# Gates from two fp32r parts, the mLSTM denominator as a value column, zero-filled differential queries, norm rows without diagonals

## The chip, the cores and the metric

One core of a Trainium2 chip. The metric is the device time of one execution in microseconds. An execution is about 2 us longer than its span from the first to the last instruction.

## What is computed

Two transformer blocks one behind the other, for one sequence of 512 tokens of width 1024, in float32. The weights are read once from HBM. Cut to what the change touches:

```python
# first block, layer A: mLSTM with a memory attention beside it
h = rmsnorm(x, norm_g)
qk, v, o, z, i_pre, f_pre, mq, mz = split_cols(h @ w_in, [...])     # i_pre, f_pre: 4 columns each
...
num = einsum("bhts,bhsv->bhtv", p, vb) + ...                         # 4 heads of 256
den = jnp.sum(p, axis=-1) + ...
h_out = num / jnp.maximum(jnp.abs(den), jnp.exp(-m_t))[..., None]
...
# second block: differential attention, 4 heads of two 64-wide components
s = einsum('bqhcd,bkhcd->bhcqk', q_blk, k) * scale
p = softmax(where(mask, s, NEG_BIG))
a = p[:, :, 0] - lam * p[:, :, 1]
...
return rms_norm(x, g_final)
```

Each layer begins with `rmsnorm(t, g) = t * rsqrt(mean(t*t) + EPS) * g`.

## The kernel before, in words

Activations stand with features on the partitions. Every large product is a sum over k-tiles of 128 features. Weights and activations are fp32; for the products each is split in two fp32r parts, hi (a copy that rounds) and lo (the rest), and one product row group is three fp32r matmuls: hi by hi, hi by lo, lo by hi (`product_rows`, L1237 to L1239 for products whose output has tokens on the partitions, L1242 to L1244 for features). Weights come in 256 to 512 KB parts by SP's DMAs into two raw slots; for each part ScalarE writes hi (L1536) and DVE lo (L1901) into one of three split slots. Everything else on PE is plain fp32.

A planner (`Plan`, `order_of_work`) lays out one list of steps in Python before anything is recorded: product row groups with their evictions, and between them side steps from two lanes, each with a lag in the planner's own clock (`lag`, `side_ns`). `tensor_program`, the ScalarE and DVE programs and POOL's then each walk this list and record their share, with semaphore waits between them.

The stages are A (the mLSTM layer), B (latent attention), C (differential attention and a pooling branch), D (cross attention), E (MLP) and the end. The steps that matter here:

- **Norms** (a, mem, b, c, m2, d, e, f): `sqa` squares a tile of x on ScalarE (L1577), `sqp` adds it to a running sum on POOL (L2454). `nsq` is four one-column fp32 matmuls (L1269) that give the sum of squares of each token. `nsum` is two small DVE operations and a power of -1/2 on POOL (L2445). `ndiag` writes four diagonal blocks with the roots on DVE (L1904), `nrow` is one fp32 matmul of ones with these (L1277), which gives the roots as a row on all partitions; ScalarE copies it to SBUF (L1580). For the last norm, f, POOL adds only tiles 1 to 3; `nsq f` takes the other four tiles as extra blocks (20 matmuls). `store` multiplies x, the gain and the row on DVE (L1910) and SP writes the result out.
- **gate0 to gate3**: the eight columns i_pre and f_pre, as 64 zero-filled columns of fp32 weights `gw`, two k-tiles per step, two fp32 matmuls per k-tile (L1297, L1298). They run between row groups of product qkA0. `gateP` and `gateA` make cumulative sums and maxima of the gates on DVE and ScalarE, `gateT` turns them on PE (L1308). After them on DVE come the evictions and the causal convolution of head 0, then the splits and the output gates of ozA0.
- **hval** (head h, token tile i): the denominator as (i+1) matmuls of the probabilities with a column of ones (L1358), the numerator as (i+1) with 256 value columns (L1360), into one bank.
- **dsc** (head h, query tile j), 16 units in stage C: for each of two components one score matmul on 64 partitions (L1428) and one mask matmul of 128 bf16 columns (L1216). Scores of 128 partitions with the same form stand in stage B (L1396).
- **rtp**: turns the rotated queries and keys of a head; ScalarE copies them out (L1791).
- **gate_loads** and **late**: side loads, the first in stage A after product mv0, the second at the start of stage C.

## Time and profile before

| | us |
|---|---|
| three runs | 1663.5, 1662.62, 1660.24 (median 1662.62) |
| the profiled execution | 1657.19 |
| its span | 1655.4 |
| PE busy in it | 1590.4 (96%) |
| DVE busy | 910.1 (55%) |
| ScalarE (ACT) busy | 692.8 (42%) |
| POOL busy | 150.6 (9%) |
| mean granted TensorE clock | 0.987 of 2.4 GHz |

The busy time of PE is that of matmuls whose ends are modelled and which overlap; the distance between starts, or the chain of waits, gives their pace. An fp32 matmul leaves two records.

### The profile page before, as it was taken

Reading aid. Unit: us, or ns where it says so; the run is one execution under the profiler, and the core shown is the slowest. Engines: PE = TensorE matmul, PEld = TensorE weight load, DVE = VectorE, ACT = ScalarE, POOL = GpSimd, SP = SyncE. Lnnn points to the kernel's source line nnn. Section 1 sums busy time; section 2 is a strip of 40 time slices with the busy share of each in tenths; the row PEclk is TensorE's granted clock in tenths of the full one; section 3 lists DMA queues with packets and bytes.
Section 4 is the critical chain, followed back from the end, with each engine's and each line's share of the span. In section 5 each row is a group of like instructions: output and inputs, shape, how many; then the busy total and the mean of one; then the engine's idle time right before and its main releaser. Section 6 shows DMA issues by size and latency. Waiting matters only on the chain.

```text
span 1655.4 us, 19328 instructions
## 1 busy us (share of the span) xinstructions
PE 1590.4 (96%) x7194; PEld 1250.7 (76%) x7194; DVE 910.1 (55%) x1856; ACT 692.8 (42%) x1587; POOL 150.6 (9%) x115
## 2 busy tenths in 40 slices
PE   7999999999999998999899999999999999999996
PEld 5867777777898876666577777688877888888885
DVE  6457485648555566466448556765554544444342
ACT  6633342323346656456334344343343433333241
POOL 3002020202110000000013000011001100000001
PEclk9999999999999999999999999999999999999998
DMA  6522121323324321012124221124232333333231
GB/s 191 151 60 77 51 77 52 93 61 125 105 75 135 87 63 47 26 53 77 51 66 127 77 65 51 52 89 140 72 108 77 98 93 102 92 99 101 90 102 51
DMA packets 90109, 141.06 MB, mean 85 GB/s; under 512 B 7456, under 2 KB 37536, under 8 KB 90016
## 3 DMA queue, kind: packets, MB, share of 16 engines
q1 hardware_dynamic: 89296, 139.02, 27.7%
q8 instruction: 57, 0.93, 0.2%
q10 hardware_dynamic: 720, 0.81, 0.2%
q14 instruction: 36, 0.29, 0.1%
HBM read 137.71 MB, written 2.10 MB: 84 GB/s over the span
## 4 chain that ended last, share of the span: by engine, by line
PE 78%; DVE 12%; ACT 5%; issue 3%; DMA 2%; POOL 0%; SPq 0%; POOLq 0%; ACTq 0%; DVEq 0%
PE banks L1237 16%; PE banks L1239 16%; PE banks L1238 16%; PE banks L1242 5%; PE banks L1244 5%; PE banks L1243 5%; DVE sb_w_split L1901 3%; DVE sb_arena L1901 3%; DVE sb_arena L1910 2%; PE banks L1200 2%; ACT sb_junk L1504 1%; PE banks L1412 1%; PE banks L1397 1%; PE banks L1360 1%; DVE sb_arena L1904 1%
## 5 line engine op out<-in xcount | busy, mean ns | idle before, releaser
L1901 DVE TENSOR_TENSOR sb_w_split<-sb_raw,sb_w_split 128x512 fp32r<-128x512 f32 (+4 forms) x530 | 342.9, 689 | 374.3 <-ACT sb_w_split L1536 373.6
L1536 ACT ACTIVATE sb_w_split<-sb_raw 128x512 fp32r<-128x512 f32 (+4 forms) x530 | 287.9, 592 | 418.7 <-PE banks L1239 314.3
L1237 PE MATMUL banks<-sb_actA,sb_w_split 128*128 128x512 f32 x672 | 278.1, 414 | 0.3 <-ACT sb_arena L1594 0.3
L1239 PE MATMUL banks<-sb_actA,sb_w_split 128*128 128x512 f32 x672 | 263.8, 393 | 0.0
L1238 PE MATMUL banks<-sb_actA,sb_w_split 128*128 128x512 f32 x672 | 263.0, 391 | 0.0
L1237 PE MATMUL banks<-sb_actB,sb_w_split 128*128 128x512 f32 (+1 forms) x640 | 249.4, 390 | 4.3 <-DVE sb_w_split L1901 2.2
L1239 PE MATMUL banks<-sb_actB,sb_w_split 128*128 128x512 f32 (+1 forms) x640 | 243.2, 380 | 0.0
L1238 PE MATMUL banks<-sb_actB,sb_w_split 128*128 128x512 f32 (+1 forms) x640 | 243.2, 380 | 0.0
L1242 PE MATMUL banks<-sb_w_split,sb_actA 128*128 128x512 f32 (+1 forms) x384 | 155.6, 405 | 15.8 <-DVE sb_w_split L1901 9.4
L1244 PE MATMUL banks<-sb_w_split,sb_actA 128*128 128x512 f32 (+1 forms) x384 | 149.8, 390 | 0.0
L1243 PE MATMUL banks<-sb_w_split,sb_actA 128*128 128x512 f32 (+1 forms) x384 | 149.6, 390 | 0.0
L1237 PEld LDWEIGHTS banks<-sb_actA,sb_w_split 128*128 128x128 f32 x672 | 127.5, 190 | 28.0 <-issue 3.6
L1239 PEld LDWEIGHTS banks<-sb_actA,sb_w_split 128*128 128x128 f32 x672 | 126.8, 189 | 27.8
L1238 PEld LDWEIGHTS banks<-sb_actA,sb_w_split 128*128 128x128 f32 x672 | 127.4, 190 | 25.2 <-issue 1.2
L1237 PEld LDWEIGHTS banks<-sb_actB,sb_w_split 128*128 128x128 f32 x640 | 121.3, 190 | 29.9 <-issue 3.6
L1238 PEld LDWEIGHTS banks<-sb_actB,sb_w_split 128*128 128x128 f32 x640 | 121.4, 190 | 22.9 <-issue 1.4
L1239 PEld LDWEIGHTS banks<-sb_actB,sb_w_split 128*128 128x128 f32 x640 | 121.2, 189 | 22.9
L2454 POOL TENSOR_TENSOR sb_arena<-sb_arena 128x512 f32<-128x512 f32 x41 | 61.2, 1492 | 696.5 <-ACT sb_arena L1577 693.9
L2445 POOL TENSOR_TENSOR sb_small<-sb_small,sb_cons 128x4 f32<-128x4 f32 (+3 forms) x30 | 42.4, 1414 | 674.8 <-DVE sb_small L1907 617.3
L1242 PEld LDWEIGHTS banks<-sb_w_split,sb_actA 128*128 128x128 f32 x384 | 73.3, 191 | 31.4 <-issue 10.5
L1200 PE MATMUL banks<-sb_cons,sb_arena 128*128 128x128 f32 x460 | 77.3, 276 | 19.6 <-DVE sb_arena L1904 9.9
L1200 PEld LDWEIGHTS banks<-sb_cons,sb_arena 128*128 128x128 f32 x460 | 57.5, 141 | 43.7 <-DVE sb_arena L1904 14.0
(185 smaller groups left out, 2076.5 us busy)
## 6 DMA issues: line engine op xcount, KB each, us to landing
sb_raw<-in_a_w_in SPq DMA_DIRECT2D x66, 256.0 KB, 3.0
sb_raw<-in_w_up SPq DMA_DIRECT2D x32, 512.0 KB, 3.7
sb_raw<-in_w_down SPq DMA_DIRECT2D x32, 512.0 KB, 3.7
sb_raw<-in_w_in SPq DMA_DIRECT2D x24, 512.0 KB, 3.6
sb_raw<-in_mem_w_kv SPq DMA_DIRECT2D x16, 512.0 KB, 3.8
sb_raw<-in_w_ckv SPq DMA_DIRECT2D x16, 512.0 KB, 3.8
sb_raw<-in_a_w_in SPq DMA_DIRECT2D x15, 512.0 KB, 3.8
sb_raw<-in_a_w_out SPq DMA_DIRECT2D x12, 512.0 KB, 3.8
```

What stands on the lines that cost most here:

```text
L1200: t = pe.op.transpose(v.ps[0:rows, place.bank, n * P:(n + 1) * P], block, v.ident)
L1237: pe.op.matmul(out, hi[:, cs], x.hi(k), start=i == 0, stop=False)
L1238: pe.op.matmul(out, hi[:, cs], x.lo(k), start=False, stop=False)
L1239: t = pe.op.matmul(out, lo[:, cs], x.hi(k), start=False, stop=last_i)
L1242: pe.op.matmul(out, x.hi(k)[:, cs], hi, start=i == 0, stop=False)
L1243: pe.op.matmul(out, x.hi(k)[:, cs], lo, start=False, stop=False)
L1244: t = pe.op.matmul(out, x.lo(k)[:, cs], hi, start=False, stop=last_i)
L1536: act.op.activation(hi[:, cs], raw[:, cs], ACT.Copy).then_inc(act.mark(m("w_hi"), 2 * n + part + 1), 1)
L1901: dve.op.tensor_tensor(out, a, b, op).then_inc(dve.mark(*mark) if mark else dve.tick(), 1)
L1910: dve.op.scalar_tensor_tensor(out=out, in0=a, scalar=s, in1=b, op0=op1, op1=op2).then_inc(dve.mark(*mark) if mark else dve.tick(), 1)
L2445: pool.op.tensor_tensor(v.stat(root, n), v.stat(mean, n), v.con("minus_half", 0, n), ALU.pow).then_inc(m.at("rstd", step)[0], 1)
L2454: pool.op.tensor_tensor(total, total, v.square_of(norm, n)[1], ALU.add).then_inc(signal, 1)
```

## The change

- Gates: `gw` is loaded as 64 dense numbers per partition by one DMA. POOL zero-fills two fp32r arrays of 1024 columns (`gw_parts`, in the free places 8 and 9 of actB), the new step `gate_split` puts hi (ScalarE) and lo (DVE) of the weights into them. Each k-tile is three fp32r matmuls, 24 in all. The planner's cost of a gate step falls from 3440 to 1360.
- hval: the values of a head are stored as 257 columns, the last of them ones, written once by POOL (`v_ones`). One matmul per source tile gives numerator and denominator. The arrays behind it move by 8 or 16 columns.
- Differential queries: two arrays, one for each component, each with the other component's 64 partitions zero. POOL fills the zeros in `late`, the turned queries are copied out in two halves. The scores run over all 128 partitions. The second array lies in places 0 to 3 of actB's lo part, so `ysplit yC` waits for the scores of its head (which the order met before as well).
- Norms: `ndiag` goes, but for the two small operations of norm a. `nrow` is four (m2: two) matmuls of the root column, read as 128 equal columns, with the identity; it takes ndiag's place in the order. `nsum` has one DVE operation. For norm f POOL adds tiles 1 to 5, nsq takes two extra blocks and waits for each by itself, and `store` reads the row from PSUM.

The core of the diff (left out: the names of signals, views that only move, and the two evictions that write values by head):

```diff
@@ -246,7 +246,7 @@
         return (i + 1) * (430 + 224)
-    return {"aval": 10 * P * wide_f32, "gate0": 3440, "gate1": 3440, "gate2": 3440, "gate3": 3440, "pp": 860,
+    return {"aval": 10 * P * wide_f32, "gate0": 1360, "gate1": 1360, "gate2": 1360, "gate3": 1360, "pp": 860,
@@ -293,7 +293,7 @@
-    return [("sqa", norm, n)] + ([("sqp", norm, n)] if n and not (norm == "f" and n >= 4) else [])
+    return [("sqa", norm, n)] + ([("sqp", norm, n)] if n and not (norm == "f" and n >= 6) else [])
@@ -495,8 +495,7 @@
         if row:
-            p.side(lane, (), ("ndiag", norm), lag=2600)
-            p.side(lane, (), ("nrow", norm), lag=2600)
+            p.side(lane, (), *([("ndiag", norm)] if norm == "a" else []), ("nrow", norm), lag=2600)
@@ -572,6 +571,7 @@
     head_norm(1, "mk0", MT, False)
+    p.side(1, (), ("gate_split",))
@@ -607,6 +607,9 @@
                 p.need(("hval", h - 1, 3))
+            else:
+                p.need(("hnsq", "mqA", TT - 1), ("hnt", "mqA", MEM_HEADS - 1))
+                p.put(("v_ones",))
@@ -771,7 +774,7 @@
         p.step()
-    for kind in ("nsq", "nsum", "ndiag", "nrow"):
+    for kind in ("nsq", "nsum", "nrow"):
@@ -868,7 +871,10 @@
         self.conv = at.take(4, SEQ)
-        self.v_sb = at.take(TT, 512)
+        self.v_sb = at.take(TT, 2 * (M_DIM + 1))
+        flat = self.v_sb.rearrange("p a b -> p (a b)")
+        self.v_heads = flat.rearrange("p (a h n) -> p a h n", a=TT, h=2)
+        mq_raw_a = flat[:, 0:2048].rearrange("p (a b) -> p a b", a=TT)
@@ -877,12 +883,13 @@
         self.gate_f = flat[:, 0:SEQ]
-        self.gw = flat[:, SEQ:].rearrange("p (k n) -> p k n", k=KD)
+        self.gw = flat[:, SEQ:SEQ + 64].rearrange("p (k n) -> p k n", k=KD)
+        self.gw_parts = [actB[:, n, 8:10, :].rearrange("p a (k n) -> p (a k) n", n=P) for n in range(2)]
...
         at.take(SEQ)
@@ -944,7 +951,7 @@
         self.scratch["c"] = self.cprob_c[0].rearrange("p a b -> p (a b)")
-        self.kTc, self.qTc = at.take(4, SEQ), at.take(4, SEQ)
+        self.kTc, self.qTc = at.take(4, SEQ), [at.take(4, SEQ), two[:, 1, 0:4, :]]
@@ -1260,21 +1267,24 @@
             if norm == "f":
-                blocks += [(v.square_of(norm, n)[1], 0) for n in range(4, KD)]
-                pe.wait_ge(*m.at("sq", ("sqa", norm, last)))
-                last = 3
+                blocks += [(v.square_of(norm, n)[1], 0) for n in (6, 7)]
+                last = 5
             pe.wait_ge(*m.at("sq_sum", ("sqp", norm, last)))
-            for i in range(tiles):
-                for n, (block, at) in enumerate(blocks):
+            for n, (block, at) in enumerate(blocks):
+                if norm == "f" and n:
+                    pe.wait_ge(*m.at("sq", ("sqa", norm, 5 + n)))
+                for i in range(tiles):
                     t = pe.op.matmul(v.ps[:, place.bank, i:i + 1], block[:, at + i * P:at + (i + 1) * P], v.con("ones", 0, 1),
-                                     start=n == 0, stop=n == len(blocks) - 1)
+                                     start=n == 0 and i == 0, stop=n == len(blocks) - 1 and i == tiles - 1)
...
         elif kind == "nrow":
-            n = v.tiles_of[a[0]] * P
-            pe.wait_ge(*m.at("diag", ("ndiag", a[0])))
+            pe.wait_ge(*m.at("rstd", ("nsum", a[0])))
             place, full = open_bank(step)
-            s = v.scratch[a[0]]
-            pe.op.matmul(v.ps[:, place.bank, 0:n], v.con("ones"), s[:, 0:n], start=True, stop=True).then_inc(full, 1)
+            r = v.stat(("r", a[0]), v.tiles_of[a[0]])
+            for i in range(v.tiles_of[a[0]]):
+                t = pe.op.matmul(v.ps[:, place.bank, i * P:(i + 1) * P], r[:, i:i + 1].broadcast_to([P, P]), v.ident,
+                                 start=True, stop=True)
+            t.then_inc(full, 1)
@@ -1288,14 +1298,16 @@
                 open_bank(step)
-                pe.wait_ge(m("dma_gate"), 32)
+                pe.wait_ge(*m.at("gw_lo", ("gate_split",)))
             place = plan.place[("gate0",), 0]
-            out = v.ps[0:64, place.bank, :]
+            out = v.ps[:, place.bank, :]
...
                 x = v.src["hA"]
-                pe.op.matmul(out, v.gw[:, k, :], x.hi(k).bitcast(F32), start=k == 0, stop=False)
-                t = pe.op.matmul(out, v.gw[:, k, :], x.lo(k).bitcast(F32), start=False, stop=k == KD - 1)
+                hi, lo = (w[:, k, :] for w in v.gw_parts)
+                pe.op.matmul(out, hi, x.hi(k), start=k == 0, stop=False)
+                pe.op.matmul(out, hi, x.lo(k), start=False, stop=False)
+                t = pe.op.matmul(out, lo, x.hi(k), start=False, stop=k == KD - 1)
@@ -1353,12 +1365,10 @@
                 pe.wait_ge(*m.evicted(f"vA{h - h % 2}", j))
-            num, dn = v.ps[:, place.bank, 0:M_DIM], v.ps[:, place.bank, M_DIM:M_DIM + 1]
+            pe.wait_ge(m("v_ones"), 1)
             for s in range(i + 1):
-                pe.op.matmul(dn, v.pT_m[:, s, i * P:(i + 1) * P], v.con("ones", 0, 1), start=s == 0, stop=s == i)
-            for s in range(i + 1):
-                t = pe.op.matmul(num, v.pT_m[:, s, i * P:(i + 1) * P],
-                                 v.v_sb[:, s, (h % 2) * M_DIM:(h % 2 + 1) * M_DIM], start=s == 0, stop=s == i)
+                t = pe.op.matmul(v.ps[:, place.bank, 0:M_DIM + 1], v.pT_m[:, s, i * P:(i + 1) * P],
+                                 v.v_heads[:, s, h % 2, :], start=s == 0, stop=s == i)
@@ -1421,11 +1431,11 @@
                 place, full = open_bank(step, c)
-                hs = slice(c * 64, c * 64 + 64)
+                pe.wait_ge(m("q_zero"), 2)
...
                 s = v.bank(place, n=ke)
-                pe.op.matmul(s, v.qTc[hs, h, qs], v.kTc[hs, h, 0:ke], start=True, stop=False)
+                pe.op.matmul(s, v.qTc[c][:, h, qs], v.kTc[:, h, 0:ke], start=True, stop=False)
@@ -1575,7 +1585,7 @@
             act.op.activation(out, src, ACT.Square).then_inc(act.mark(*m.at("sq", step)), 1)
-        elif kind == "nrow":
+        elif kind == "nrow" and a[0] != "f":
@@ -1639,6 +1651,12 @@
             act.op.activation(sg, v.out_of(name, j), ACT.Tanh, scale=0.5).then_inc(act.mark(*m.at("sig", step)), 1)
+        elif kind == "gate_split":
+            hi = v.gw_parts[0].rearrange("p k (c n) -> p k c n", n=32)[:, :, 0:2, 0:4]
+            act.wait_ge(m("dma_gate"), 16)
+            act.wait_ge(m("gw_zero"), 2)
+            act.op.activation(hi, v.gw.rearrange("p k (c n) -> p k c n", c=2), ACT.Copy
+                              ).then_inc(act.mark(*m.at("gw_hi", step)), 1)
@@ -1788,8 +1806,11 @@
             src, place, empty = bank(step)
-            act.op.activation((v.kTc if x == "k" else v.qTc)[:, h, :], src,
-                              ACT.Copy).then_inc(act.mark(empty, place.after), 1)
+            if x == "k":
+                act.op.activation(v.kTc[:, h, :], src, ACT.Copy).then_inc(act.mark(empty, place.after), 1)
+            else:
+                act.op.activation(v.qTc[0][0:64, h, :], src[0:64, :], ACT.Copy).then_inc(act.tick(), 1)
+                act.op.activation(v.qTc[1][64:P, h, :], src[64:P, :], ACT.Copy).then_inc(act.mark(empty, place.after), 1)
@@ -1974,21 +1995,12 @@
             src, place, empty = bank(("nsq", norm), n=n)
-            s = v.stat(("s", norm), n)
-            scalar(s, src, 1.0 / D_MODEL, ALU.mult, empty, place.after)
-            dve.settle()
-            scalar(v.stat(("ms", norm), n), s, EPS, ALU.add, *m.at("ms", step))
+            both(v.stat(("ms", norm), n), src, 1.0 / D_MODEL, ALU.mult, EPS, ALU.add, empty, place.after)
         elif kind == "ndiag":
-            norm = a[0]
-            n = v.tiles_of[norm]
-            r, diag = v.stat(("r", norm), n), v.scratch[norm]
-            dve.wait_ge(*m.at("rstd", ("nsum", norm)))
-            if norm == "a":
-                scalar(v.stat("half_r", n), r, 0.5, ALU.mult)
-                scalar(v.stat("quarter_r", n), r, 0.25, ALU.mult)
-            for i in range(n):
-                scalar(diag[:, i * P:(i + 1) * P], v.ident, r[:, i:i + 1], ALU.mult,
-                       *(m.at("diag", step) if i == n - 1 else ()))
+            r = v.stat(("r", "a"), TT)
+            dve.wait_ge(*m.at("rstd", ("nsum", "a")))
+            scalar(v.stat("half_r", TT), r, 0.5, ALU.mult)
+            scalar(v.stat("quarter_r", TT), r, 0.25, ALU.mult, *m.at("parts_r", step))
@@ -2069,6 +2083,10 @@
                   *m.at("silu", step))
+        elif kind == "gate_split":
+            hi, lo = (w.rearrange("p k (c n) -> p k c n", n=32)[:, :, 0:2, 0:4] for w in v.gw_parts)
+            dve.wait_ge(*m.at("gw_hi", step))
+            tensor(lo, v.gw.rearrange("p k (c n) -> p k c n", c=2), hi.bitcast(F32), ALU.subtract, *m.at("gw_lo", step))
@@ -2405,9 +2425,8 @@
             k = a[0]
-            dve.wait_ge(*m.emptied(("nrow", "f")))
-            fused(v.out_sb[:, k, :], v.x_res[:, k, :], v.col("g_final", k), ALU.mult, v.row["f"], ALU.mult,
-                  *m.at("out", step))
+            row = bank(("nrow", "f"))[0]
+            fused(v.out_sb[:, k, :], v.x_res[:, k, :], v.col("g_final", k), ALU.mult, row, ALU.mult, *m.at("out", step))
@@ -2441,7 +2460,7 @@
             mean, root, n = root_of(step)
-            pool.wait_ge(*m.at("ms", step))
+            pool.wait_ge(*(m.emptied(("nsq", a[0])) if kind == "nsum" else m.at("ms", step)))
@@ -2451,13 +2470,24 @@
             total = v.sq_sum[norm]
-            pool.op.tensor_tensor(total, total, v.square_of(norm, n)[1], ALU.add).then_inc(signal, 1)
+            pool.op.tensor_tensor(total, total, v.square_of(norm, n)[1], ALU.add).then_inc(pool.mark(signal, value), 1)
...
         elif kind == "gate_loads":
-            pool.op.memset(v.gw, 0.0).then_inc(m("gw_zero"), 1)
+            for n in range(2):
+                pool.op.tensor_scalar(v.gw_parts[n], v.ident.unsqueeze(1).broadcast_to([P, KD, P]), 0.0, None,
+                                      ALU.mult).then_inc(m("gw_zero"), 1)
...
                 pool.op.memset(v.u_pad[:, u, 0:CONV_W - 1], 0.0).then_inc(m("pads"), 1)
+        elif kind == "late":
+            pool.settle()
+            pool.op.memset(v.qTc[0][64:P, :, :], 0.0).then_inc(pool.mark(m("q_zero"), 1), 1)
+            pool.settle()
+            pool.op.memset(v.qTc[1][0:64, :, :], 0.0).then_inc(m("q_zero"), 1)
+        elif kind == "v_ones":
+            pool.wait_ge(*m.full(("hnt", "mqA", MEM_HEADS - 1)))
+            pool.wait_ge(*m.at("sums", ("hnsq", "mqA", TT - 1)))
+            pool.op.memset(v.v_heads[:, :, :, M_DIM:], 1.0).then_inc(m("v_ones"), 1)
@@ -2493,9 +2523,7 @@
             w = io["a_w_in"][:, A_IG:A_IG + 8].rearrange("(k p) n -> p k n", p=P)
-            sp.wait_ge(m("gw_zero"), 1)
-            sp.op.dma_start(v.gw[:, :, 0:4], w[:, :, 0:4]).then_inc(m("dma_gate"), 16)
-            sp.op.dma_start(v.gw[:, :, 32:36], w[:, :, 4:8]).then_inc(m("dma_gate"), 16)
+            sp.op.dma_start(v.gw, w).then_inc(m("dma_gate"), 16)
```

What the planner makes of it, at three places. **DVE, stage A, around the gates' sums.** `4x512` rows are gateP and gateA, `sb_w_split` the splits, `banks,sb_arena 128x512 x4` the evictions that begin the convolution. Before:

```order
L1910 SCALAR_TENSOR_TENSOR sb_x_res<-sb_arena,sb_x_res 128x512
L1901 TENSOR_TENSOR sb_arena<-banks,sb_arena 4x512 x2
L1904 TENSOR_SCALAR sb_arena<-sb_arena,sb_cols 4x512 x2
L1904 TENSOR_SCALAR sb_arena<-sb_arena 4x512
L2116 TENSOR_REDUCE sb_small<-banks 128x1
L1904 TENSOR_SCALAR sb_small<-sb_small 128x1
L1901 TENSOR_TENSOR sb_arena<-sb_arena 4x512
...
L1901 TENSOR_TENSOR sb_arena<-sb_arena 4x512
L1901 TENSOR_TENSOR sb_w_split<-sb_raw,sb_w_split 128x512 x2
L2122 RECIPROCAL sb_small<-sb_small 128x1
L1904 TENSOR_SCALAR sb_arena<-sb_arena,sb_small 128x256
...
L1901 TENSOR_TENSOR sb_w_split<-sb_raw,sb_w_split 128x512 x2
L1901 TENSOR_TENSOR sb_arena<-banks,sb_arena 128x512 x4
```

And now:

```order
L1931 SCALAR_TENSOR_TENSOR sb_x_res<-sb_arena,sb_x_res 128x512
L2134 TENSOR_REDUCE sb_small<-banks 128x1
L1925 TENSOR_SCALAR sb_small<-sb_small 128x1
L1922 TENSOR_TENSOR sb_arena<-banks,sb_arena 4x512 x2
L1925 TENSOR_SCALAR sb_arena<-sb_arena,sb_cols 4x512 x2
L1925 TENSOR_SCALAR sb_arena<-sb_arena 4x512
L1922 TENSOR_TENSOR sb_w_split<-sb_raw,sb_w_split 128x512 x2
L1922 TENSOR_TENSOR sb_arena<-sb_arena 4x512
...
L1922 TENSOR_TENSOR sb_arena<-sb_arena 4x512
L2140 RECIPROCAL sb_small<-sb_small 128x1
L1925 TENSOR_SCALAR sb_arena<-sb_arena,sb_small 128x256
...
L1922 TENSOR_TENSOR sb_w_split<-sb_raw,sb_w_split 128x512 x2
L1922 TENSOR_TENSOR sb_arena<-banks,sb_arena 128x512 x4
```

The split of two parts that stood behind gateA stands now between gateP and gateA, and the reduction of the first memory score ahead of gateP.

**POOL, at the start of stage C** (the `128x512` rows are the additions of norm c, then of m2; the small ones the powers). The change alone:

```order
L2464 TENSOR_TENSOR sb_small<-sb_small,sb_cons 128x8 x8
L2473 TENSOR_TENSOR sb_arena<-sb_arena 128x512 x4
L2484 MEMSET sb_arena 64x2048
L2486 MEMSET sb_actB_plain 64x2048
L2473 TENSOR_TENSOR sb_arena<-sb_arena 128x512 x3
L2464 TENSOR_TENSOR sb_small<-sb_small,sb_cons 128x4
L2473 TENSOR_TENSOR sb_actB_plain<-sb_actB_plain 128x512 x3
```

The two fills stand between the fourth and the fifth addition of norm c; before, its seven additions followed each other.

**PE, the end.** Before:

```order
L1237 MATMUL banks<-sb_actB,sb_w_split 128x512
L1238 MATMUL banks<-sb_actB,sb_w_split 128x512
L1239 MATMUL banks<-sb_actB,sb_w_split 128x512
L1269 MATMUL banks<-sb_cons,sb_arena 128x1 x20
L1277 MATMUL banks<-sb_arena,sb_cons 128x512
```

And now:

```order
L1244 MATMUL banks<-sb_actB,sb_w_split 128x512
L1245 MATMUL banks<-sb_actB,sb_w_split 128x512
L1246 MATMUL banks<-sb_actB,sb_w_split 128x512
L1277 MATMUL banks<-sb_cons,sb_arena 128x1 x12
L1285 MATMUL banks<-sb_cons,sb_small 128x128 x4
```

Twenty one-column matmuls became twelve, and the row four matmuls with `sb_small`, which holds the roots.

## Rows read from the trace of the kernel before

**Rows 1.** the page: busy time, share of the span, instructions of the engines

```profile
PE 1590.4 (96%) x7194; PEld 1250.7 (76%) x7194; DVE 910.1 (55%) x1856; ACT 692.8 (42%) x1587; POOL 150.6 (9%) x115
```

**Rows 2.** the chain of waits: start us, us, what; a gate pair, products

```profile
97.04 1.00 PE banks L1297 x2
98.04 0.86 PE banks L1298 x2
...
994.89 0.23 PE banks L1238
```

**Rows 3.** timeline of DVE, 105 to 150: start us, us, instructions [idle before]

```profile
105.81 1.39 DVE L1901 TENSOR_TENSOR sb_arena<-banks,sb_arena 4x512 f32<-4x512 f32 x2 [6.12 <-PE banks L1298]
...
142.12 2.35 DVE L1901 TENSOR_TENSOR sb_w_split<-sb_raw,sb_w_split 128x512 fp32r<-128x512 f32 x2 [3.39 <-ACT sb_w_split L1536]
...
148.50 0.41 DVE L1910 SCALAR_TENSOR_TENSOR sb_arena<-sb_arena,banks 128x256 f32<-128x256 f32 x1
```

**Rows 4.** timeline of PE at 149 and 309

```profile
149.05 0.47 PE L1242 MATMUL banks<-sb_w_split,sb_actA 128*128 128x512 f32 x1 [2.46 <-DVE sb_arena L1910]
...
309.06 0.77 PE L1242 MATMUL banks<-sb_w_split,sb_actA 128*128 128x512 f32 x1 [3.30 <-DVE sb_arena L1910]
```

**Rows 5.** busy time in two stretches: PE, PEld, DVE, ACT, POOL, PEclk, DMA

```profile
1024.00:1053.00 29.00, 28.34 (x138) 20.82 (x137) 26.86 (x79) 10.57 (x34) 1.01 (x1) 1.00 0.18 55
309.00:312.00 3.00, 2.94 (x7) 2.40 (x8) 2.86 (x8) 2.21 (x4) 0.00 (x0) 0.50 0.79 292
```

**Rows 6.** the chain of waits, last hval step of head 0

```profile
200.29 0.78 PE banks L1358 x8
201.07 1.83 PE banks L1360 x8
```

**Rows 7.** the chain of waits: scores of 64 rows, then of 128 (L1396)

```profile
961.01 0.11 PE banks L1200
...
992.18 1.05 PE banks L1428 x2
993.23 0.16 PE banks L1216
...
999.56 0.41 PE banks L1428 x2
...
687.35 0.86 PE banks L1396 x2
```

**Rows 8.** timeline of all engines, norm b

```profile
484.13 0.95 PE L1269 MATMUL banks<-sb_cons,sb_arena 128*128 128x1 f32 x8
...
487.06 1.45 POOL L2445 TENSOR_TENSOR sb_small<-sb_small,sb_cons 128x4 f32<-128x4 f32 x1 [4.49 <-DVE sb_small L1904]
```

**Rows 9.** timeline of POOL: a memset, three additions of norm c

```profile
45.84 0.53 POOL L2458 MEMSET sb_arena<- 128x512 f32 x1
...
879.24 4.78 POOL L2454 TENSOR_TENSOR sb_arena<-sb_arena 128x512 f32<-128x512 f32 x3 [4.69 <-ACT sb_arena L1577]
```

**Rows 10.** timeline of PE at 39

```profile
39.31 0.47 PE L1242 MATMUL banks<-sb_w_split,sb_actB 128*128 128x512 f32 x1 [1.25 <-DVE sb_w_split L1901]
```

**Rows 11.** timeline of all engines, the end

```profile
1635.94 0.63 ACT L1577 ACTIVATE sb_arena<-sb_x_res 128x512 f32<-128x512 f32 x1 [0.73 <-DVE sb_x_res L1901]
...
1636.67 5.50 PE L1269 MATMUL banks<-sb_cons,sb_arena 128*128 128x1 f32 x40 [1.49 <-issue]
...
1642.66 1.02 POOL L2445 TENSOR_TENSOR sb_small<-sb_small,sb_cons 128x4 f32<-128x4 f32 x1 [20.59 <-DVE sb_small L1904]
1643.71 0.87 DVE L1904 TENSOR_SCALAR sb_arena<-sb_cons,sb_small 128x128 f32<-128x128 f32 x4 [1.13 <-POOL sb_small L2445]
...
1644.64 2.08 PE L1277 MATMUL banks<-sb_arena,sb_cons 128*128 128x512 f32 x2 [2.46 <-DVE sb_arena L1904]
...
1647.38 5.39 DVE L1910 SCALAR_TENSOR_TENSOR sb_arena<-sb_x_res,sb_cols,sb_arena 128x512 f32<-128x512 f32 x8 [2.80 <-ACT sb_arena L1580]
```

**Rows 12.** groups by form, DVE: count, busy us, mean ns, idle before

```profile
L1910 DVE SCALAR_TENSOR_TENSOR sb_arena<-banks,sb_arena 128x512 f32<-128x512 f32 x48 | 32.9, 689 | 52.3 <-PE banks L1412 27.1 <-PE banks L1239 10.6 <-PE banks L1331 8.1
```

22 lines of the change are left out of this document (14 added, 8 removed).

## The prediction

> **What bounds the kernel now.** I read the page first. PE is busy 96% of a span of 1655.4 us [rows 1], so a microsecond taken from PE counts unless another engine is waited for at that place. The chain of waits then gives the pace of single matmuls, which the busy durations overstate because matmuls overlap: an fp32r product record of 512 columns takes 0.23 us, two fp32 records 0.86 [rows 2]. (An fp32 matmul leaves two records in the trace.) The timelines of DVE and POOL show where PE depends on them, and the windows show the granted clock.
>
> **Gates in two parts.** Before, sixteen fp32 matmuls, one per k-tile and part of hA, in groups of 8, 4 and 4. Each takes 0.86 us, the first of a group 1.00 [rows 2]: 13 x 0.86 + 3 x 1.00 = 14.2 us. Now 24 fp32r matmuls of the products' own form: 24 x 0.23 = 5.5. PE gives up 8.7 us.
>
> Not all of it arrives. After the gates DVE runs gateP and gateA and then the convolution of head 0, from 105.81 on. ScalarE has little to do and waits for DVE; it makes the next weights' first parts only behind a softmax step that needs DVE, and DVE's split at 142.12 waits 3.39 for it. DVE then reaches the output gate at 148.50 [rows 3], for whose bank PE had waited 2.46 us at 149.05 [rows 4]. So between 105.81 and 149.05 a chain of DVE and ScalarE sets the end, and what counts is when it starts. Before, 6 row groups of product work (3 matmuls, 0.68 us each) stood between the first gate at 87.0 and the end of the fourth. Now, by the planner's order, 10 stand there (4 of them ahead of gate0), and one memory score of 0.45: 87.0 + 6.8 + 0.45 + 5.5 = 99.8. The chain starts at 99.8 in place of 105.8, 6.0 earlier. Within it a split of two parts (1.2 us) now stands ahead of gateA, where it waits for ScalarE, which is at the logarithm of gateP; before, it stood behind gateA. I count 0.8 as lost by that: gateA begins one ScalarE copy and one split later (0.6 + 1.3 + hand-over, 2.0), and the 1.2 of the split behind it are saved. **Gates: -5.2 us**, between -8.7 (everything arrives) and -3.5 (a longer PE wait brings the clock down: after a wait of 3.3 at 309.06 the window 309 to 312 ran at 0.50, 1.2 GHz [rows 4, 5], which over 3.4 us costs 1.7). The two new steps gate_split are 64 elements per partition on ScalarE and DVE, 0.2 us each, three row groups ahead of their reader: nothing.
>
> **Denominator as a value column.** The last of the four hval steps of a head takes 0.78 for 8 one-column records and 1.83 for the 8 value records [rows 6]. Per head there are 20 such one-column records, 80 in all: 80 x 0.098 = 7.8 us go. The value records grow from 256 to 257 columns: 80 x 0.23/256, under 0.1. PE has no wait next to these steps, and the longer DVE-bound stretches begin after them. **-7.6**, between -6.5 and -7.8.
>
> **Differential queries on 128 rows.** One unit (dsc) does two score matmuls, each followed by a mask. With 64 rows and 512 columns two records take 1.05; a 128-row score matmul of the same columns, in layer B, takes 0.86 [rows 7]. With 128 columns it is 0.41 against twice the 0.11 of a 128-row record [rows 7]: 0.19 again, whatever the columns. So 32 x 0.19 = 6.1 us. The mask behind a 64-row matmul takes 0.16 [rows 7], for 128 columns of bf16; if its excess comes from the change of row count it shrinks too, by nothing at least and 0.10 at most: I take 0.07 x 32 = 2.2. PE gives up 8.3. From 1024 to 1053 DVE is busy 26.86 of 29 us [rows 5], filled by the pooling windows, and there PE already waits; three of the 16 units lie there, so 3/16 is lost. **-6.8**, between -8.6 and -5.0.
>
> The Trainium skill ("TensorE: Matmul & The Clock Gate", the part on loading weights) says of this that timing follows the column count and "row count K doesn't matter here"; by that rule this part brings nothing. Rows 7 speak against it as far as pairs of records go.
>
> **Norm rows without diagonals.** One fp32 matmul of 512 columns (0.86) becomes four of 128, at 0.11 a record 0.88: even. Gone are 24 DVE operations on diagonals, beside PE work everywhere except at the end. But nrow now stands where ndiag stood, earlier on PE. In layer B, nsq ends at 485.08, four row groups of 384 columns follow (12 x 0.23 x 384/512 = 2.1 us), PE arrives at 487.2 and the root is ready at 488.51, minus 0.2 for the DVE operation saved [rows 8]: **+1.1**, between +0.5 and +2. In the other stages product work of 512 columns covers it; for m2 the new wait replaces one that follows anyway.
>
> **Zero fills on POOL.** The first one writes 2 x 1024 columns at 45.8, where a memset of 512 took 0.53 [rows 9]. It reads its input, so its cost lies between memset pace (2.1 us for both) and that of the fp32 additions beside it (4.78 for three of 512 columns, so 6.4 us for both). DVE's splits read two operands from SBUF, and beside POOL's additions a pair took 2.35 in place of 1.3 [rows 3]. PE had waited 1.25 for a split at 39.31 [rows 10], so cover here is thin: **+1.0**, between 0 and +4.7. The second, 2 x 2048 columns on 64 partitions between the additions of norm c, costs at memset pace 2 x 2.1 = 4.2 and falls into 4.69 us in which POOL waited for ScalarE [rows 9]: nothing; if it ran longer, PE's nsq c would be late by the excess.
>
> The Trainium skill ("SBUF — State Buffer", section "Who interferes with whom") says that a VectorE instruction with two SBUF inputs contends with a GpSimd one that reads SBUF, and not with one that only writes it. By that rule the first fill could hold a split back by the length of one fill, and the second touches nobody.
>
> **The end.** PE ran 40 one-column records in 5.50 us from 1636.67, after the last square [rows 11]. Now additions 4 and 5 are POOL's (about 1.4 each, done by 1635.4), 16 records run before the last square is needed at 1636.57 and 8 after it. At 0.11 a record nsq ends near 1638.2 instead of 1642.17: -4.0. One of two small DVE operations: -0.2. The diagonals (0.87 plus hand-over): -0.95. The row itself took 2.08 at the low clock, where such a pair takes 0.86 elsewhere, and becomes 8 records of 0.11 to 0.21, 0.9 to 1.7: -0.7. ScalarE's copy with its hand-overs, from 1646.72 to 1647.38: -0.65. The stores read PSUM instead of SBUF; fused DVE operations with a bank operand take 0.69 a piece [rows 12], so 8 of them stay at 5.4 to 5.5. **-6.4**, between -4.5 and -7.5.
>
> **Sum:** -5.2 - 7.6 - 6.8 + 1.1 + 1.0 - 6.4 = **-23.9 us**. The profiled execution took 1657.19, so 1633.3 for such a one; the three runs lie higher (median 1662.62), and I forecast against that median: **1639 us**. The bounds add to -13 (3.5, 6.5, 5.0, 4.5 against 2 and 4.7) and -32 (8.7, 7.8, 8.6, 7.5 against 0.5), neither likely at once.
>
> **The rivals.**
> (A) Row count costs nothing in itself and the 0.19 follows the fp32 score matmul wherever it stands. For it: the other 128-row scores stand among other instructions. The rule of the Trainium skill told above says the same. Against it: every 64-row record, in layer B too, is longer by the same amount whatever its columns. Without this term: 1639 + 6.8 = 1646.
> (B) PE stops being the bound. DVE and ScalarE chains absorb the PE time in the mLSTM and differential stretches: half of 19.6 us is lost, 1649. For it: DVE at 26.86 of 29 us in one stretch. Against it: elsewhere DVE idles waiting for PE.
> (C) Slower. The value operand of every second head now starts at an odd column and is 257 wide. If TensorE read such an operand at a fraction of the pace, the 80 value records (0.23 each) would pay. It decides from (23.9/80) = 0.30 us more per record, that is at 2.3 times the present; at four times it is 80 x 0.69 = 55 us, 1694. Nothing in the profile has an odd width on PE.
> (D) More arrives than I let: the gates whole and no price for the fill, 1634 or less.
> That the gate matmuls don't become faster (the same data as fp32r) is excluded well enough by the products, which use exactly this form.
>
> **How the numbers follow.** Forecast as told 0.60, A 0.08, B 0.14, C 0.03, D 0.15. The range 1630 to 1649 leaves out C and the cases in which nearly all upper or all lower bounds hold at once. 0.2% is 3.3 us, about what a measurement of this kernel can tell from no change. Same needs 20 us of the sum to be missing, A and B together: 0.03. Slower is C: 0.03. Faster: 0.94.
>
> **What would show it.** Gates: 24 records a 0.23 us apart; gateP on DVE 5 to 6 us sooner than 105.8; a PE wait ahead of the output-gate products near 113 and a longer one near 144. Value column: no one-column records in hval, value records still 0.23. Scores: pairs of 0.86 with 128 rows. Layer B: a PE wait of about 1 us before the norm row. First fill: two POOL rows of 1 to 3 us and a DVE split stretched beside them. End: from the last square to the first store about 4.4 us, before 10.8. The prediction is wrong if 128-row scores keep 1.05, if value records are longer, or if PE's idle time grows by more than some 8 us.

## The result, and the profile after

The changed kernel takes **1637.53 us** (median of 4 runs, 1633.78 to 1638.79) against 1662.81 for the kernel before beside it: ratio 0.9847, 95% interval 0.9828 to 0.9866. The profiled execution took 1637.44 (span 1635.6, mean granted clock 0.982), 19.8 less than the profiled one of before, whose time lay 5.6 below its median. The same kernel, run again on another occasion (e1), gave 0.9862 (0.9843 to 0.9882) and a profiled execution of 1635.2. One execution of a later kernel, e4, took 2106 us at a mean granted clock of 0.699, and is left out of every ratio.

PE, from the page of the changed kernel ([rows 1] is the line of before):

```profile
PE 1569.4 (96%) x7128; PEld 1249.8 (76%) x7128; DVE 903.4 (55%) x1823; ACT 694.7 (42%) x1591; POOL 160.9 (10%) x121
q8 instruction: 56, 0.92, 0.2%
```

PE's busy time fell by 21.0 us. The second line, a DMA queue of 56 blocks that hold instructions, is used further down.

**Where the time went.** Both kernels have 5712 product records in nearly the same order, so the k-th record of one can be set beside the k-th of the other. This is how far the changed kernel is ahead (minus) at seven such records and at the end, in us, and the step since the last one, worked out from the two traces, and the same for e1:

| product record, its time before | changed | step | e1 | step | forecast of the step |
|---|---|---|---|---|---|
| 150th, 49.9 us (start, first fill) | +1.93 | +1.93 | +0.14 | +0.14 | +1.0 |
| 480th, 149.1 (gates) | -3.37 | -5.30 | -4.89 | -5.03 | -5.2 |
| 1500th, 465.5 (value column) | -12.29 | -8.92 | -13.85 | -8.96 | -7.6 |
| 1767th, 516.2 (norm row of layer B) | -8.98 | +3.31 | -8.85 | +5.00 | +1.1 |
| 3000th, 943.4 (the rest up to the scores) | -7.73 | +1.25 | -8.11 | +0.74 | 0 |
| 3400th, 1089.1 (scores) | -14.01 | -6.28 | -15.95 | -7.84 | -6.8 |
| 5700th, 1632.3 | -14.83 | -0.82 | -16.95 | -1.00 | 0 |
| end of the span | -19.8 | -4.97 | -22.0 | -5.05 | -6.4 |

The gates, from the chain of waits of the changed kernel (start us, us, what): the last three gate records, 0.23 apart, and gateP behind them. [rows 2] had 0.86 for a pair of records.

```profile
101.02 0.23 PE banks L1308
101.25 0.23 PE banks L1309
101.47 0.24 PE banks L1310
101.71 0.02 issue
101.74 0.68 DVE sb_arena L1922
```

gateP starts at 101.74 in place of 105.81 [rows 3], on a trace that was 1.9 late by then: 6.0 sooner net. DVE behind it (timeline of DVE) waits for ScalarE ahead of gateA and again ahead of the split at 138.75, and reaches the output gates at 145.12 in place of 148.50 [rows 3]:

```profile
101.74 1.39 DVE L1922 TENSOR_TENSOR sb_arena<-banks,sb_arena 4x512 f32<-4x512 f32 x2 [2.10 <-PE banks L1310]
107.97 1.29 DVE L1922 TENSOR_TENSOR sb_w_split<-sb_raw,sb_w_split 128x512 fp32r<-128x512 f32 x2 [3.38 <-ACT sb_w_split L1546]
109.37 0.68 DVE L1922 TENSOR_TENSOR sb_arena<-sb_arena 4x512 f32<-4x512 f32 x1
138.75 2.35 DVE L1922 TENSOR_TENSOR sb_w_split<-sb_raw,sb_w_split 128x512 fp32r<-128x512 f32 x2 [3.39 <-ACT sb_w_split L1546]
145.12 0.41 DVE L1931 SCALAR_TENSOR_TENSOR sb_arena<-sb_arena,banks 128x256 f32<-128x256 f32 x1
```

PE's waits, from its timeline. Those at 115 and 118 are new, and that at 145.68 stands where 2.46 stood [rows 4]. The norm rows of b and m2 (L1285) wait now. (At 17.23 PE waited 1.80, before 1.35.)

```profile
115.11 0.62 PE L1320 MATMUL banks<-sb_cons,sb_arena 4*128 4x4 f32 x8 [0.69 <-DVE sb_arena L1922]
117.95 0.77 PE L1249 MATMUL banks<-sb_w_split,sb_actA 128*128 128x512 f32 x1 [2.22 <-DVE sb_arena L1922]
145.68 0.47 PE L1249 MATMUL banks<-sb_w_split,sb_actA 128*128 128x512 f32 x1 [0.78 <-DVE sb_arena L1931]
477.26 1.16 PE L1285 MATMUL banks<-sb_cons,sb_small 128*128 128x128 f32 x8 [2.25 <-POOL sb_small L2464]
899.20 0.71 PE L1285 MATMUL banks<-sb_cons,sb_small 128*128 128x128 f32 x4 [1.98 <-POOL sb_small L2464]
```

And three stretches of the changed kernel by windows (us, then busy PE, PEld, DVE, ACT, POOL, then PE's granted clock, DMA share, GB/s):

```profile
18.00:22.00 4.00, 4.00 (x12) 3.13 (x11) 4.00 (x4) 2.41 (x5) 3.14 (x3) 0.57 0.75 252
117.00:124.00 7.00, 6.05 (x15) 4.79 (x16) 6.86 (x14) 2.59 (x8) 0.00 (x0) 0.52 0.27 78
1622.50:1627.60 5.10, 3.75 (x17) 3.36 (x16) 0.16 (x1) 0.00 (x0) 1.02 (x1) 0.50 0.00 0
```

0.50 is the lower level of the clock, 1.2 GHz: it holds in nearly all of the first two stretches and in the whole third one, each time behind a PE wait or one-column work.

The value column and the scores, from the chain of waits (beside [rows 6] and [rows 7]): 8 value records in 1.73, no denominator, and a unit of two 512-column score pairs, each with its mask.

```profile
195.62 1.73 PE banks L1370 x8
...
957.66 0.86 PE banks L1438 x2
958.52 0.06 PE banks L1223
958.57 0.91 PE banks L1438 x2
959.49 0.06 PE banks L1223
```

The end, from the timelines of PE, ACT, DVE and POOL ([rows 11] before):

```profile
1620.62 3.55 PE L1277 MATMUL banks<-sb_cons,sb_arena 128*128 128x1 f32 x24 [0.27 <-POOL sb_arena L2473]
1621.12 0.63 ACT L1587 ACTIVATE sb_arena<-sb_x_res 128x512 f32<-128x512 f32 x1 [0.73 <-DVE sb_x_res L1922]
1624.20 0.16 DVE L1928 TENSOR_SCALAR sb_small<-banks 128x4 f32<-128x4 f32 x1 [3.12 <-PE banks L1277]
1624.45 1.02 POOL L2464 TENSOR_TENSOR sb_small<-sb_small,sb_cons 128x4 f32<-128x4 f32 x1 [3.97 <-DVE sb_small L1928]
1625.52 2.08 PE L1285 MATMUL banks<-sb_cons,sb_small 128*128 128x128 f32 x8 [1.35 <-POOL sb_small L2464]
1627.63 0.75 DVE L1931 SCALAR_TENSOR_TENSOR sb_arena<-sb_x_res,sb_cols,banks 128x512 f32<-128x512 f32 x1 [3.27 <-PE banks L1285]
```

From the end of the last square (1621.75) to the first `store` step on DVE (1627.63): 5.88 us, before 10.8.

### The profile page after: what moved, and what is told of

It reads as the page before. It is cut to its first block, busy times and chain, and to the rows that moved or that the text cites. A ratio compares the mean times of both kernels' runs of the same rounds, so it can differ in the third digit from the quotient of the medians.

```text
span 1635.6 us, 19180 instructions
## 1 busy us (share of the span) xinstructions
PE 1569.4 (96%) x7128; PEld 1249.8 (76%) x7128; DVE 903.4 (55%) x1823; ACT 694.7 (42%) x1591; POOL 160.9 (10%) x121
## 4 chain that ended last, share of the span: by engine, by line
PE 78%; DVE 12%; ACT 5%; issue 2%; DMA 2%; POOL 1%; SPq 0%; POOLq 0%; DVEq 0%; ACTq 0%
PE banks L1244 16%; PE banks L1246 16%; PE banks L1245 16%; PE banks L1249 5%; PE banks L1251 5%; PE banks L1250 5%; DVE sb_w_split L1922 3%; DVE sb_arena L1922 3%; DVE sb_arena L1931 2%; PE banks L1207 2%; ACT sb_junk L1514 1%; PE banks L1422 1%; PE banks L1407 1%; ACT sb_w_split L1546 1%; PE banks L1370 1%
## 5 line engine op out<-in xcount | busy, mean ns | idle before, releaser
L1692 ACT ACTIVATE sb_arena<-banks,sb_small 128x256 f32<-128x256 f32 (+2 forms) x80 | 45.4, 568 | 107.6 <-DVE sb_small L1925 107.4
```

The costliest lines, as they stand in the source:

```text
L1692: act.op.activation(prob, src, ACT.Exp, bias=v.soft("mx", step, 1), scale=scale, accum_out=v.soft("sm", step, 1)).then_inc(act.mark(empty, ...
```

## The experiments

Twelve more kernels ran: e1 is the changed one as it stands, the others are edited from it. Ratios are to the kernel before, run beside them.

**e1: the changed kernel again.**

> The changed kernel once more, nothing edited, as the measure for the other runs on this chip and for how much one execution differs from another. In its profiled execution PE ran at the low clock from 18.2 to 21.6 us and was 1.9 us late by 50 us; before was not. Theory: that is chance of the execution (the wait at 17 us was 0.45 longer than before, and the first 47 us hold no instruction that the change adds), so it is missing in some executions. Rival: the new order of transfers or the fill causes it, then it shows again with the same 1.8 to 2 us. Time 1637.5 within 3.

Measured: 1637.36 us (4 runs), 0.9862 (0.9843 to 0.9882). PE waited 1.05 at 17.04, and the clock stayed up, by windows:

```profile
18.00:22.00 4.00, 4.00 (x19) 3.27 (x19) 4.00 (x4) 2.41 (x6) 3.14 (x3) 1.00 0.70 237
```

19 records ran in the four microseconds in which 12 had run. At the 150th product record e1 is 0.14 behind the kernel before, and all eleven later kernels lie within 0.5 of it too. The 1.9 us of the first profiled execution were chance of that execution; below, e1 is the measure. The length of the wait alone does not decide it: in e8 PE waited 1.78 at 16.90, as long as in that execution, and the clock stayed up (1.00 from 17 to 22).

**e2: 64-row scores.**

```diff
-                pe.wait_ge(m("q_zero"), 2)
+                hs = slice(c * 64, c * 64 + 64)
...
-                pe.op.matmul(s, v.qTc[c][:, h, qs], v.kTc[:, h, 0:ke], start=True, stop=False)
+                pe.op.matmul(s, v.qTc[c][hs, h, qs], v.kTc[hs, h, 0:ke], start=True, stop=False)
```

> The changed kernel with the differential scores on 64 rows again (same tiles, same fills and copies, only the operands cut to the 64 rows that hold numbers). Theory: the row count itself costs about 0.27 us per score matmul with its mask, 32 of them, 8.6 us of PE, of which some 2 us fall into places where PE waits for DVE anyway: 6 to 7 us slower than e1, records of 512 columns at 1.05 us a pair in place of 0.86, masks at 0.16 in place of 0.09. Rival (row count does not matter, as a rule of the Trainium skill has it): within 1 us of e1 and pairs of 0.86.

Measured: 1645.28 (5 runs), 0.9906 (0.9889 to 0.9923), 7.9 slower than e1. The same unit in its chain of waits:

```profile
961.68 1.05 PE banks L1438 x2
962.73 0.16 PE banks L1223
962.89 1.05 PE banks L1438 x2
963.95 0.16 PE banks L1223
```

Nothing but the number of rows differs, so the row count is what costs. In the first pair of a unit, from start to start, the first record takes 533 ns with 64 rows and 432 with 128 at 512 columns, and 214 against 111 at 128 columns: 0.10 us whatever the columns. With 64 rows the second pair (partitions 64 to 127) takes 533 again; with 128 its first record takes 485. The mask behind the first pair takes 0.16 in place of 0.06, and the 128-row record just ahead of a unit 0.20 in place of 0.11. So the cost lies on the 64-row records and on their neighbours, 0.54 us a unit in all. Between the 3000th and the 3400th product record e2 loses 7.9 us to e1.

The Trainium skill ("TensorE: Matmul & The Clock Gate", on loading weights) says of the weight load that its time follows the columns and that "row count K doesn't matter here". The loads themselves agree: their records are 0.18 to 0.19 us long with 64 rows and with 128. But the distance between matmul records does not follow the loads alone. The prediction had carried the sentence over to the whole part; read so, it would have left e2 within 1 us of e1. Rival A of the prediction falls.

**e3: the denominator apart.**

```diff
-            for s in range(i + 1):
-                t = pe.op.matmul(v.ps[:, place.bank, 0:M_DIM + 1], v.pT_m[:, s, i * P:(i + 1) * P],
-                                 v.v_heads[:, s, h % 2, :], start=s == 0, stop=s == i)
+            num, dn = v.ps[:, place.bank, 0:M_DIM], v.ps[:, place.bank, M_DIM:M_DIM + 1]
+            for s in range(i + 1):
+                pe.op.matmul(dn, v.pT_m[:, s, i * P:(i + 1) * P], v.con("ones", 0, 1), start=s == 0, stop=s == i)
+            for s in range(i + 1):
+                t = pe.op.matmul(num, v.pT_m[:, s, i * P:(i + 1) * P],
+                                 v.v_heads[:, s, h % 2, 0:M_DIM], start=s == 0, stop=s == i)
```

> The changed kernel with the denominator as a matmul of its own again (80 more records of one column, value records 256 columns wide, of the same value tile with its stride and its odd start for every second head). Theory: the traces differ by 8.9 us over the four heads, 0.11 us for each record, not the 0.098 that I forecast: 8.9 us slower than e1. Rival: the forecast of 7.6. A third: the width 257 or the odd start costs something in the changed kernel; then the value records here are shorter than 0.23 apart and the loss is under 7.

Measured: 1643.64 (6 runs), 0.9902 (0.9885 to 0.9919), 6.3 slower than e1. Between the 480th and the 1500th record e3 lost 10.1 us to e1. Of this 1.2 lie behind the wait that ends at 304, where the clock stayed low until 310 (in e1 from 299.5 to 303), and 8.9 at the hval steps. Added up from the traces, the sixteen hval steps take 23.4 us in the kernel before and in e3, and 14.5 in the changed kernel and in e1. Within hval the value records stand 0.216 us apart in the changed kernel (257 columns) as they did before (256, [rows 6]); width and odd start cost nothing that these records show, and rival C falls. But by the 1767th record e3 is only 6.3 behind e1: layer B gave 4.0 us back. That led to the next finding.

**Why layer B gave time back.** PE's wait ahead of the norm row was 2.42 in e1 and 1.02 in e3 (timelines of PE):

```profile
475.87 1.16 PE L1285 MATMUL banks<-sb_cons,sb_small 128*128 128x128 f32 x8 [2.42 <-POOL sb_small L2464]
```
```profile
484.75 0.93 PE L1285 MATMUL banks<-sb_cons,sb_small 128*128 128x128 f32 x6 [1.02 <-POOL sb_small L2467]
```

The DVE read of the norm's sums stands behind a split that waits for ScalarE, which waits for a weight transfer (timeline of DVE and ScalarE, e1; then ScalarE of e3):

```profile
471.97 0.83 ACT L1546 ACTIVATE sb_w_split<-sb_raw 128x320 fp32r<-128x320 f32 x2 [5.12 <-DMA sb_raw<-in_w_kv_a]
472.47 0.89 DVE L1922 TENSOR_TENSOR sb_w_split<-sb_raw,sb_w_split 128x320 fp32r<-128x320 f32 x2 [2.22 <-ACT sb_w_split L1546]
...
474.12 0.15 DVE L1928 TENSOR_SCALAR sb_small<-banks 128x4 f32<-128x4 f32 x1
```
```profile
480.85 0.83 ACT L1549 ACTIVATE sb_w_split<-sb_raw 128x320 fp32r<-128x320 f32 x2 [3.73 <-DMA sb_raw<-in_w_kv_a]
```

SP issued that transfer 2.63 us ahead of nsq in every kernel. From the issue to ScalarE's start, and PE's wait:

| kernel | before | e3 | e11 | changed | e1 | e4 | e8 | e6 | e10 | e12 | e2 |
|---|---|---|---|---|---|---|---|---|---|---|---|
| landing, us | 2.97 | 2.93 | 4.07 | 4.16 | 4.33 | 4.46 | 4.48 | 4.74 | 4.79 | 4.98 | 5.05 |
| wait, us | none | 1.02 | 2.17 | 2.25 | 2.42 | 2.56 | 2.57 | 2.83 | 2.88 | 3.06 | 3.14 |

In the three kernels whose row stands elsewhere and does not wait, the landing is 4.01 (e9), 4.75 (e7) and 5.20 (e5). The wait is the landing less 1.9, within 0.02, in all ten kernels that have it. And the DMA queues between issue and landing (queue, kind: packets, MB, share of 16 engines), in e1 and then in e3:

```profile
q1 hardware_dynamic: 538, 0.65, 49.0%
q8 instruction: 1, 0.02, 1.5%
```
```profile
q1 hardware_dynamic: 272, 0.33, 36.4%
```

A block of instructions (16 KB on one DMA engine, 0.9 to 1.9 us) was under way beside the weights in each of the twelve traces with a late landing, and in neither of the two with an early one. Before, blocks came at 465 and at 491, beside an issue at 481.5. In the changed kernel one comes at 470.2, 1.0 us behind the issue at 469.2, and in e3, which gives PE 80 records back, they come at 462 and at 489, beside an issue at 477.9. ScalarE started 1.2 to 1.9 us behind the end of the block. That the change moved the block into the transfer because PE has fewer instructions ahead of it, and that the block holds up the weights' last packets on its DMA engine, is my reading of this coincidence; no run moved the block alone. The Trainium skill ("Runtime: NRT & Kernel Launch", section "Instruction fetch mechanics") has the instructions come in such 16 KiB blocks through a DMA queue of their own and calls the cost "mostly hidden"; if my reading holds, it was not hidden here.

**e4: fp32 gates.** The diff in short: weights in one fp32 tile, memset and two transfers as before, and

```diff
-                pe.op.matmul(out, hi, x.hi(k), start=k == 0, stop=False)
-                pe.op.matmul(out, hi, x.lo(k), start=False, stop=False)
-                t = pe.op.matmul(out, lo, x.hi(k), start=False, stop=k == KD - 1)
+                pe.op.matmul(out, v.gw[:, k, :], x.hi(k).bitcast(F32), start=k == 0, stop=False)
+                t = pe.op.matmul(out, v.gw[:, k, :], x.lo(k).bitcast(F32), start=False, stop=k == KD - 1)
```

> The changed kernel with the gates in fp32 on 64 columns again, with the zero fill by memset, the two transfers behind it, no two-part weights, and the planner's cost for a gate step of before (so its order there too). Theory: 5.2 us slower than e1 (the DVE chain behind the gates starts about 6 us later and gains 0.8 by its order), the last gate ends near 105, and the wait of about 2.4 us at the head's last rows is back. Rival: everything that PE gave up arrives, 8.7 slower. Another: the fill had cost 2 us near 50; then only 3 slower.

Measured: 1644.27 (the median of 5 runs; 1644.1 without the one of 2106), 0.9899 (0.9880 to 0.9917), 6.9 slower than e1. At the 480th record it is 5.05 behind e1; then the clock fell behind PE's wait at its output gates, and at the 600th it is 6.7 behind. Of 8.7 us that PE gave up, 5 arrive, as forecast. At the 150th record e4, without the fill, is level with e1 (0.10 behind).

**e8: the first fill twice.**

```diff
-            for n in range(2):
+            for i, n in enumerate((0, 1, 0, 1)):
+                if i > 1:
+                    pool.wait_ge(m("gw_zero"), i - 1)
```

> The changed kernel with the first zero fill written twice (four operations of 2.8 us on POOL in place of two, from 46 to 57). I had forecast 1.0 us for the fill, up to 4.7. Theory: it costs nothing in place of 1.0: it lies beside DVE splits that keep their 0.68 to 0.69 us a piece, and nobody waits for POOL there, so twice the fill is within 1 us of the changed kernel too and DVE's splits stay at 0.69. Rival (VectorE with two SBUF inputs is held back by a GpSimd operation that reads SBUF): the splits beside it grow towards the 1.2 of those beside POOL's additions, PE waits for them, and the time grows by 1 to 3 us.

Measured: 1639.64 (4 runs), 0.9851 (0.9825 to 0.9876): no difference that the runs can tell. In the traces e8 keeps its distance from the kernel before within 0.1 us from the 40th to the 280th product record (21 to 82 us), and all four fills lie in that stretch. POOL, and the first two of the four DVE pairs beside it (the other two took 1.29 each), from the timelines:

```profile
45.58 11.01 POOL L2480 TENSOR_SCALAR sb_actB<-sb_cons 128x1024 fp32r<-128x1024 f32 x4
```
```profile
46.59 1.29 DVE L1922 TENSOR_TENSOR sb_w_split<-sb_raw,sb_w_split 128x512 fp32r<-128x512 f32 x2 [1.78 <-ACT sb_w_split L1546]
49.12 1.40 DVE L1922 TENSOR_TENSOR sb_w_split<-sb_raw,sb_w_split 128x512 fp32r<-128x512 f32 x2 [1.23 <-ACT sb_w_split L1546]
```

2.75 us for 1024 columns is near the pace of the additions (3.2), the upper end of my bounds; but a DVE pair beside it stays at 1.3 to 1.4, where one beside the additions took 2.35 [rows 3]. In the first trace of the changed kernel the pairs beside the fill took 1.35 and 1.49. The rule of the Trainium skill ("SBUF — State Buffer", section "Who interferes with whom"), by which a VectorE instruction with two SBUF inputs contends with a GpSimd one that reads SBUF, would have held these pairs back; this fill, whose one input is a block of 128 columns read eight times, hardly did. Whether that is for the single input or for something else in its form, no run tells.

**e11: squares 4 and 5 on PE.** In `squares` `n >= 6` becomes `n >= 4`, and `nsq` takes four blocks of single squares in place of two.

> The changed kernel with squares 4 and 5 of the last norm summed by PE again, not by POOL (40 one-column records in place of 24), in the changed kernel's order by square, so that only the last waits. Theory: PE starts them 0.3 us sooner, right behind its last product, 16 records of 0.11 to 0.21 more follow, and the clock falls in their midst: the first store 2 to 3 us later than in the changed kernel. Rival: the additions on POOL are what PE waits for, the extra records lie in that time: within 0.5 us.

Measured: 1639.95 (4 runs), 0.9872 (0.9855 to 0.9888). Timeline of PE:

```profile
1622.88 6.05 PE L1277 MATMUL banks<-sb_cons,sb_arena 128*128 128x1 f32 x40
```

The first store comes 7.96 us after the last square, in e1 5.77: the additions on POOL are worth 2.2 us. In e4 the clock happened to stay up through nsq and nearly all of the row, and the same step took 4.37 us, with nsq in 2.81 and the row in 1.29, where the changed kernel took 3.55 and 2.08. So the low clock costs this end up to 1.5 us.

**e5 and e9: the norm row later.** e5 for b and m2:

```diff
+            if norm != "a":
+                p.side(lane, (), lag=2600)
             p.side(lane, (), *([("ndiag", norm)] if norm == "a" else []), ("nrow", norm), lag=2600)
```

> The changed kernel with the norm rows of b and m2 a further 2600 ns of planned work behind the root, where they stood before the change (norm a and f unchanged). In two profiled executions of the changed kernel PE waited 2.25 and 2.42 us ahead of the norm row in layer B, and between the rows ahead of it and 507 us it lost 3.3 and 5.0 us against before. Theory: the early place costs that: 2.3 us of wait, and 1.7 more in executions in which the clock falls behind it, so 2.5 to 4 us faster than the changed kernel, and no wait ahead of that row. Rival: layer B waits for its weights and gives the same time back at the next wait (near 498 and 506); then within 1 us. Norm m2: nothing, one wait takes the other's place.

e9 with `if norm == "b"`:

> The changed kernel with the norm row of layer B alone later (m2 stays as changed). With both later the median fell to 1631.9, 5.5 below the changed kernel's, where the trace gives 3.5 us to layer B and up to 2.9 to the stretch around m2 (there by a fall of the clock at 900 us that is missing). Theory: b is the larger part and m2 matters too: 3 to 4 us faster than the changed kernel, some 1634, and PE waits 1.98 us ahead of the norm row of m2. Rival (my forecast: m2's new wait takes the place of one that follows anyway): all is in b, so 1632.

Measured: e5 1631.92 (5 runs), 0.9817 (0.9799 to 0.9835); e9 1633.39 (4 runs), 0.9833 (0.9819 to 0.9848). Neither has a PE wait over 0.25 us ahead of the row in layer B, and they gained 3.3 and 4.1 us on e1 between the 1500th and the 1767th record, though their weights landed 5.20 and 4.01 us after their issue. (Against the first trace of the changed kernel, where the clock stayed up there, e5 gained 1.6 and e9 2.4.) In the groups of PE between 460 and 520 us of e5:

```profile
L1287 PE MATMUL banks<-sb_cons,sb_small 128*128 128x128 f32 x8 | 1.2, 288 | 0.2 <-POOL sb_small L2466 0.2
```

So the early place was needed for the loss; late weights without it cost PE no wait at the row. What m2's row adds (1.5 us in the medians, within the intervals) is not settled.

**e6, e10, e12: ScalarE's copies earlier.** On ScalarE alone, in place of `for step in plan.order`:

```diff
+    order = list(plan.order)
+    for late, n in ((("gateP",), 21), (("exp", "msc", "A", 0, 3), 25)):
+        order.remove(("split", n))
+        order.insert(order.index(late), ("split", n))
+    for step in order:
```

> The changed kernel with two of ScalarE's weight copies earlier on ScalarE alone: split 21 ahead of gateP, split 25 ahead of the exponential of memory score A 0 3 (DVE keeps its order). In the changed kernel DVE idles 3.4 us at 103 and 3.4 us at 134 because these copies stand behind a logarithm, and behind a softmax step and four tanh. Theory: a chain of DVE and ScalarE sets the end between the gates and the output gates of head 0, so it ends 3 to 4 us sooner, PE's waits at 113 to 117 shrink by 2, and 2 to 3.5 us arrive at the end. Rival: DVE's time is not what PE waits for there (PE is bound by its own work and by the low clock that it ran at from 115 to 122): the waits move, and under 0.7 us arrives.

e10 has the first of the two pairs only:

> The changed kernel with only the first of the two earlier ScalarE copies, split 21 ahead of gateP. Both together gave 8 us. Theory: the chain runs through both idle stretches of DVE, so this one alone gives about half of what the trace showed by 144 us (5.7 us): DVE's idle of 3.4 at 103 shrinks to 1.4, PE's waits at 113 and 116 shrink by 2, and 2.5 to 4 us arrive. Rival: the second stretch, at 134, sets the end of the chain alone, since the convolution lies between the two; then under 1 us.

and e12 the second only:

> The changed kernel with only the second of the two earlier ScalarE copies, split 25 ahead of the exponential of memory score A 0 3. The first alone brought nothing that could be measured: PE's wait only moved to 143, where it lasted 3.6 us. Theory: the stretch at 134 sets the end of the chain, and the first copy only pays once it is gone: this one alone takes DVE's idle of 3.4 us at 134 away and brings 3 to 4 of the 8 us that both gave, some 1634. Rival 1: it brings all of it, 1629.5. Rival 2: each alone brings nothing, 1637.

Measured: e6 **1629.35** (4 runs), 0.9804 (0.9786 to 0.9822); e10 1638.05, 0.9866 (0.9849 to 0.9883); e12 1636.23, 0.9847 (0.9819 to 0.9876). Each alone brings nothing that can be measured, both together 8 us. PE's waits over 0.4 us between 112 and 148 us in e10, then in e12, then in e6:

```profile
114.94 0.47 PE L1249 MATMUL banks<-sb_w_split,sb_actA 128*128 128x512 f32 x1 [1.19 <-DVE sb_arena L1926]
142.65 0.47 PE L1249 MATMUL banks<-sb_w_split,sb_actA 128*128 128x512 f32 x1 [3.61 <-DVE sb_arena L1935]
```
```profile
114.18 0.62 PE L1320 MATMUL banks<-sb_cons,sb_arena 4*128 4x4 f32 x8 [0.69 <-DVE sb_arena L1926]
117.02 0.77 PE L1249 MATMUL banks<-sb_w_split,sb_actA 128*128 128x512 f32 x1 [2.22 <-DVE sb_arena L1926]
```
```profile
114.16 0.47 PE L1249 MATMUL banks<-sb_w_split,sb_actA 128*128 128x512 f32 x1 [1.19 <-DVE sb_arena L1926]
```

And the windows of e10, e12 and e6 from 112 to 148:

```profile
112.00:148.00 36.00, 31.20 (x140) 25.06 (x139) 31.70 (x59) 15.17 (x33) 10.32 (x9) 0.95 0.26 74
```
```profile
112.00:148.00 36.00, 33.09 (x145) 26.84 (x144) 33.00 (x62) 15.57 (x33) 9.85 (x9) 0.91 0.26 74
```
```profile
112.00:148.00 36.00, 34.81 (x162) 28.41 (x161) 32.44 (x59) 16.89 (x37) 10.05 (x9) 1.00 0.30 89
```

In e10 PE reaches the output gates early and waits 3.61 for the second half of the chain, behind which the clock falls. In e12 the second half is short, but PE's waits at 114 and 117 stay and bring the clock down (0.91), so that PE itself is late. The two limits show in e5 too: behind the same waits as in e1 (0.70 and 2.22) the clock happened to stay up, and PE then waited 3.64 at the output gates. Only in e6 are both gone: no wait at 143, clock 1.00, 162 PE records in the stretch. By the 480th record e6 is 5.9 us ahead of e1, measured from the 150th; its median gained more than that, its one trace less (3.0 at the end, with low clock at other places). The second idle stretch of DVE, 3.38 in e1, is 1.41 in e6.

**e7: e5 and e6 together.**

> Both edits of the two runs before together. Theory: they lie in different stages, so their gains add: 5 to 7 us faster than the changed kernel, some 1631. Rival: what is gained in layer A is given back in layer B, where weights land at their own pace: then no faster than the better of the two.

Measured: **1627.7** (4 runs, 1623.07 to 1629.43), 0.9787 (0.9766 to 0.9807), the fastest of all and 9.7 below the changed kernel. The gains do not add in full (5.5 and 8.0), but neither is given back: by traces e7 leads e1 by 5.9 at the 600th record, by 8.9 at the 1767th and by 7.0 at the 5700th.

## Why the prediction was right, point by point

The forecast of 1639 and its sum of -23.9 hold against -25.3 and -22.9 by the two pairs of medians, and -19.8 and -22.0 by the traces. The terms held less well than their sum, and that it fits so closely is in part luck: the value column brought 1.3 more than forecast and the fill cost 1.0 less, while layer B cost 2.2 to 3.9 more and the end brought 1.4 less.

**Gates, -5.2: right**, -5.3 and -5.0 by the traces. gateP came 6.0 sooner, as worked out, on a trace 1.9 late. Both expected waits are there, but not in their expected sizes: 0.69 and 2.22 at 115 and 118 for the one near 113, and 0.78 at the output gates, where I had looked for the longer one. I had priced a fall of the clock only in the bound of -3.5. It came in both traces: behind the new waits the clock is low from 117 to 124, so that PE is nearly as late as the chain, and neither limit alone can be lifted with profit (e10, e12).

**Value column, -7.6: mis-sized**, -8.9. The mechanism and the size are shown (e3: 8.9 at the hval steps). My 0.098 per record came from dividing 0.78 by 8; the 8 value records behind them took 1.83 [rows 6] where they now take 1.73, so a tenth of a microsecond per group belonged to the removed records: 80 x 0.11.

**Scores, -6.8: right.** PE gives up 0.54 us in 14 of the 16 units and 0.34 in one; ahead of the last it waits, longer than before (1.32 against 0.66). With 0.54 for that one too this makes 8.4, where I had 8.3. I let 3/16 be lost in the stretch that DVE bounds; in e1 7.8 arrived, in the first trace 6.3.

**Norm row of layer B, +1.1: the step that failed.** The stretch lost 3.3 and 5.0. I took the time from nsq's end to the root from one trace (485.08 to 488.51, 3.4 us), and with it my arithmetic holds: in e3, where the weights land as early as before, the wait is 1.02. But DVE's read stands behind a split that waits for weights, and these landed 1.2 and 1.4 us later in the two traces of the changed kernel, and 1.0 to 2.2 later over all its variants but e3. That makes 2.25 and 2.42 of wait, and up to 3.14 in the variants; in e1 the clock fell behind it as well (0.85 from 470 to 480). The forecast did not name two smaller waits behind it either: 0.97 and 0.38 at 498 and 506 (e1: 0.93 and 0.40), where the kernel before had one of 0.83 at 515; e5 and e9 have them too. I had named what ends the wait, not what stands ahead of the instruction that ends it. For m2 I said the wait would take another's place: 1.98 came and the next fell from 2.09 to 0.40, as said.

**First fill, +1.0: nothing** (e8, e1), although its length, 5.5, was near the upper of the two paces that I had set, 6.4. Second fill: the two took 1.81 each and PE's wait for nsq c went from 0.56 to 0.42 in the changed kernel: nothing, as forecast, though no run left this fill out.

**The end, -6.4: mis-sized**, -5.0. From the last square to the first store I expected 4.4 and 5.88 came. With the clock up (e4) the step takes 4.37, so what I had left out is the clock: it fell in the midst of the 24 records (3.55 in place of 2.81), and the row, for which I had counted 0.7 off its 2.08, took 2.08 again in place of 1.29. One sentence of mine was wrong without changing the sum: PE started the records behind POOL's additions, 1.13 us ahead of the last square's end, so not 16 of them ran before that square was there, but some ten.

**The rest.** PE gave up some 26 us ahead of the last norm (8.7 + 8.9 + 8.4), and 14.8 and 17.0 arrived. Ahead of the last norm PE's idle in gaps over 0.25 us grew from 51.4 to 55.8 us (e1: 55.2). By an estimate from the mean clocks, 0.987 and 0.982, the low clock cost 0.013 x 1655 = 21.5 us before and 0.018 x 1636 = 29.4 now (e1, at 0.984: 26.1). Freed PE time turned into short waits and into the slower clock behind them. Rival B had the form of this, with half of the 19.6 us of gates, values and scores lost. It falls: these three steps of the table brought 20.5 and 21.8. Of the 26 us 9 to 11 were lost, most of it where the terms had allowed for it or in layer B.

## What to carry to other kernels

When work is taken from the bounding engine, look at each short wait that this opens: it costs its own length and often the clock behind it, and two limits that stand one behind the other must both be moved before either pays. When a wait is added, follow the instruction that ends it back through its own engine's queue to the transfers, and size the wait by how late these can land in several traces, not by one. A matmul on half the rows is not half the work: zero-filled to 128 rows these fp32 pairs became shorter.

## What the runs showed of the hardware

- A first fp32 matmul record on 64 rows takes 0.10 us more than on 128, at 128 columns as at 512, and the bf16 mask behind the pair and the record ahead of it 0.1 more each; the weight loads are no longer (e2).
- An operand of 257 columns that starts at an odd column runs at the pace of 256 (0.216 us a record).
- A block of instructions beside a weight transfer went with a landing 1.0 to 2.2 us later in all 12 traces with the block, and the 2 without had the early landing. No run moved the block alone.
- POOL writing zeros from one SBUF operand (2.75 us for 1024 columns) leaves DVE's two-operand splits at 1.3 to 1.5 us a pair; POOL's additions stretch them to 2.35.
- One-column matmuls in a row did not keep the clock up: in the changed kernel and in e1 it fell while the 24 records of the last norm were running back to back, in e4 behind them.
- A wait does not by its length alone decide the clock: behind waits of 0.70 and 2.22 us at 113 and 116 it fell in e1 and stayed up in e5, and behind 1.8 us at 17 it fell in the first trace of the changed kernel and stayed up in e8.
